# Modulation chunks 4 to 9 placed between the tiles of the gate projection and in the chunk loop of the recurrence

## What is computed

```python
mod_lat = jax.nn.silu(c) @ w_ada[l] + b_ada[l]        # 6 x 1024 values; the same for c_ctx
sh1, sc1, g1, sh2, sc2, g2 = jnp.split(mod[:, None, :].astype(x.dtype), 6, axis=-1)
h = rms_norm(x, lw['norm_pre1']) * (1 + sc1) + sh1
proj = h @ lw['w_in']                                 # hy, q, k, v, og, lr
...
la_f = jax.nn.log_sigmoid(lrf[..., :GLA_RANK] @ w2_f + b_f) / GLA_GATE_NORM
o_f, s_f = gla_scan(qh, kh, vh, la_f, s0_f)           # and backwards
o = rms_norm(o_f + o_b[:, ::-1], gnorm)
o = o.reshape(B, L, GLA_VAL) * jax.nn.silu(og)
...
mix = jnp.concatenate([y_hy, y_gla], axis=-1) @ lw['w_out']
x = x + g1 * rms_norm(mix, lw['norm_post1'])
h2 = rms_norm(x, lw['norm_pre2']) * (1 + sc2) + sh2
```

## Time and profile before

| | us |
|---|---|
| median of 3 runs | 2315.78 |
| lowest and highest of the 3 | 2309.94, 2328.16 |
| the profiled execution, its own time | 2312.32 |
| the profiled execution, its span in the trace | 2310.5 |

### The profile page before, as it was taken

One profiled execution on the slowest core, in us unless ns is written; L12 is line 12 of the kernel. 1 busy time (PEld: TensorE's weight loads), 2 busy tenths in 40 slices (PEclk: granted clock), 3 DMA queues, 4 the chain that ended last, 5 costly groups with the idle time before them and its releaser, 6 DMA issues.

```text
span 2310.5 us, 30679 instructions
## 1 busy us (share of the span) xinstructions
PE 2174.2 (94%) x9868; PEld 1663.6 (72%) x9868; DVE 1439.6 (62%) x3055; ACT 624.0 (27%) x930; POOL 797.5 (35%) x713
## 2 busy tenths in 40 slices
PE   6999989598998899999989999999999999999998
PEld 2554444445997787787868777787888888888886
DVE  4222322623889999788868877324766666666665
ACT  2111022233212222333323323223322323223232
POOL 0000001002323555799979999101221222212210
PEclk8999998798999999999999999999999999999999
DMA  9122134105102444599988999755988888888883
GB/s 339 41 73 73 42 109 153 64 35 191 62 13 96 155 141 136 165 292 296 301 268 288 302 284 301 233 202 184 359 287 289 292 285 294 287 287 294 285 292 145
DMA packets 293477, 475.54 MB, mean 206 GB/s; under 512 B 148871, under 2 KB 150055, under 8 KB 292872
## 3 DMA queue, kind: packets, MB, share of 16 engines
q1 hardware_dynamic: 256520, 340.20, 44.6%
q0 software_dynamic: 36864, 134.23, 16.4%
HBM read 401.76 MB, written 72.61 MB: 205 GB/s over the span
## 4 chain that ended last, share of the span: by engine, by line
PE 64%; POOL 9%; DVE 5%; issue 2%; DMA 2%; ACT 1%; SPq 1%; DVEq 0%; ACTq 0%; POOLq 0%
PE ps L959 30%; PE ps L900 19%; POOL eB L1846 6%; PE ps L837 3%; POOL ugat L1815 3%; PE ps L872 2%; PE ps L873 2%; PE ps L940 2%; PE ps L719 1%; SPq L523 1%; DMA ugat<-in_u_rows,idx 1%; DMA uraw<-in_u_t 1%; PE ps L861 1%; PE ps L819 0%; DVE h2T L1293 0%
## 5 line engine op out<-in xcount | busy, mean ns | idle before, releaser
L900 PE MATMUL ps<-h2hi,uhi 128*128 128x512 f32 x1024 | 449.1, 439 | 23.4 <-POOL ulo L1803 8.3
L900 PE MATMUL ps<-h2hi,ulo 128*128 128x512 f32 x1024 | 405.5, 396 | 0.0
L959 PE MATMUL ps<-vhi,whi 128*128 128x512 f32 x1024 | 399.8, 390 | 5.2 <-DVE wlo L1467 5.2
L900 PE MATMUL ps<-h2lo,uhi 128*128 128x512 f32 x1024 | 403.6, 394 | 0.0
L959 PE MATMUL ps<-vlo,whi 128*128 128x512 f32 x1024 | 399.7, 390 | 0.0
L959 PE MATMUL ps<-vhi,wlo 128*128 128x512 f32 x1024 | 399.5, 390 | 0.0
L1823 POOL DMA_INDIRECT vgat<-in_v_tab,idx x128 | 149.8, 1170 | 654.7 <-DVE y L1477 504.8
L1846 POOL TENSOR_SCALAR eB<-iota,jcur 128x128 f32<-128x128 f32 x384 | 315.9, 836 | 15.9 <-DVE jcur L1432 14.0
L1465 DVE TENSOR_TENSOR vlo<-vraw,vhi 128x1024 fp32r<-128x1024 f32 x128 | 156.8, 1225 | 216.3 <-ACT vhi L1739 216.3
L1739 ACT ACTIVATE vhi<-vraw 128x1024 fp32r<-128x1024 f32 x128 | 135.5, 1061 | 464.4 <-PE ps L959 462.0
L940 PEld LDWEIGHTS ps<-eA,eB 128*128 128x128 f32 x1024 | 189.8, 189 | 90.0 <-POOL eB L1846 29.9
(11 more groups left out here) (270 smaller groups left out, 2908.7 us busy)
## 6 DMA issues: line engine op xcount, KB each, us to landing
uraw<-in_u_t SPq DMA_DIRECT2D x128, 512.0 KB
vraw<-in_v_tab SPq DMA_DIRECT2D x128, 512.0 KB
gelu_scratch<-aout SPq DMA_DIRECT2D x128, 256.0 KB
gate_scratch<-gst SPq DMA_DIRECT2D x16, 2048.0 KB
ain<-gelu_scratch SPq DMA_DIRECT2D x128, 256.0 KB, 4.2
gin<-gate_scratch SPq DMA_DIRECT2D x128, 256.0 KB, 4.4
wring<-in_w_ada SPq DMA_DIRECT2D x12, 2048.0 KB, 7.8
wring<-in_w_in SPq DMA_DIRECT2D x6, 2048.0 KB, 8.4
```

The lines of the kernel that those rows point to most:

```text
L900: last = pe.matmul(ps[:, b % 4, :], w[:, b % 2, k, :], h[:, k, LP:T], start=(k == 0 and j == 0), stop=(k == KD - 1 and j == 2))
L959: last = pe.matmul(ps[:, y_bank(t) + h, :], w[:, b, (t - 1) * P:t * P], v[:, b, h * 512:(h + 1) * 512], start=(start and j == 0), stop=(st ...
```

## The change

On PE the six chunks no longer stand in one block ahead of the gate projection. Chunks 4 and 5 stay where they were, followed by two tiles of the gate projection, the columns of 4 and 5, chunks 6 and 7, the other three tiles, and the columns of 6 and 7. Chunks 8 and 9 move to the chunk loop of the recurrence, one behind the attention blocks of chunk 0 and one behind those of chunk 1, and their columns behind those of chunks 2 and 3. The gate projection's weights are loaded two places earlier in the ring. ACT moves the rows of chunks 4 and 5 ahead of its Exp and Ln, those of 6 and 7 behind the second Silu tile, and those of 8 and 9 behind the `kT` moves. DVE takes chunks 8 and 9 inside its masking loop. Since `modrow` is now in use until then, the final state `st_out`, which shared its place, gets another one, which it shares with the top-k values `sval`; so the wait for the store of the state moves from ACT (ahead of chunk 10) to DVE (ahead of the first scores).

```diff
-        st_out = at("st_out", 36, [P, 2, 2, 128])
+        st_out = at("st_out", 196, [P, 2, 2, 128])
...
-        loads += [("ada", i) for i in range(ADA_1, ADA_2)] + [("in", W_OG), ("out", 0), ("out", 512)]
+        loads += [("ada", 4), ("ada", 5), ("in", W_OG)] + [("ada", i) for i in range(6, ADA_2)] + [("out", 0), ("out", 512)]
...
@@ TensorE @@
-            for i in range(ADA_1, ADA_2):
-                ada(i)
-                if i > ADA_1:
-                    ada_cols(i - 1)
-            ada_cols(ADA_2 - 1)
-            by_token("og", ("in", W_OG))
+            ada(4)
+            ada(5)
+            by_token("og", ("in", W_OG), range(2))
+            ada_cols(4)
+            ada_cols(5)
+            ada(6)
+            ada(7)
+            by_token("og", ("in", W_OG), range(2, NT))
+            ada_cols(6)
+            ada_cols(7)
...
                     last.then_inc(bank_full, 1)
+                if c < 2:
+                    ada(8 + c)
+                elif c < 4:
+                    ada_cols(6 + c)
                 if c:
                     chunk_out(c - 1)
@@ VectorE @@
-            for i in range(4, 5):
-                modulation(i)
+            modulation(4)
...
-            for i in range(6, ADA_2):
-                modulation(i)
+            modulation(6)
+            modulation(7)
...
                 dve.wait_ge(am_ready, c + 1)
+                if c >= 3:
+                    modulation(5 + c)
...
             dve.wait_ge(h2lo_ready, NT)
+            dve.wait_ge(stored, 16)
@@ ScalarE @@
+            mod_row(4)
+            mod_row(5)
             act.wait_ge(ax_ready, 1)
             seq(act.activation(eq[:], eq[:], ACT.Exp, scale=-1.0))
             act.activation(eq[:], eq[:], ACT.Ln, bias=1.0).then_inc(ln_done, 1)
-            for i in range(4, 7):
-                mod_row(i)
...
-            for i in range(7, ADA_2):
-                mod_row(i)
             for t in range(NT):
                 move(f"og{t}", og_sb[:, t], func=ACT.Silu)
+                if t == 1:
+                    mod_row(6)
+                    mod_row(7)
             for c in range(NT):
                 move(f"kT{c}", keT[:, c].rearrange("p j n -> p (j n)"))
+            mod_row(8)
+            mod_row(9)
...
-                    if t == ADA_2:
-                        act.wait_ge(stored, 16)
                     mod_row(t)
```

More of the change, by code:

```diff
@@ L260, in bass_hybrid_layer @@
         order += [f"la{j}{s}" for j in range(4) for s in "ps"]
-        for i in range(ADA_1, ADA_2):
-            order += [f"ada{i}"] + ([f"adc{i - 1}"] if i > ADA_1 else [])
-        order += [f"adc{ADA_2 - 1}"]
-        order += [f"og{t}" for t in range(NT)]
+        order += ["ada4", "ada5", "og0", "og1", "adc4", "adc5", "ada6", "ada7", "og2", "og3", "og4", "adc6", "adc7"]
         order += [f"kT{c}" for c in range(NT)]
@@ L267, in bass_hybrid_layer @@
         for c in range(NT):
-            order += [f"at{c}0", f"at{c}1"] + ([f"o{c - 1}"] if c else [])
+            order += [f"at{c}0", f"at{c}1"] + {0: ["ada8"], 1: ["ada9"], 2: ["adc8"], 3: ["adc9"]}.get(c, [])
+            order += [f"o{c - 1}"] if c else []
         order += [f"o{NT - 1}"]
@@ L711, in _, with by_token @@
                      [(wtile(l)[:, k, (c % 4) * P:(c % 4 + 1) * P], hT[:, k, 0:LP], hT[:, k, LP:T]) for k in range(KD)])
-            def by_token(name, l):
+            def by_token(name, l, tiles=range(NT)):
                 wait_w(pe, l)
-                for t in range(NT):
+                for t in tiles:
                     u = f"{name}{t}"
```

## The result

The changed kernel takes 2286.72 us, the median of 6 runs (2281.27 to 2296.66), against 2314.65 us for the kernel before (6 runs, 2308.77 to 2328.16). The ratio is 0.988, with a 95% interval of 0.984 to 0.991. The profiled execution took 2292.26 us.

The account below looks back on a forecast made before the run. PE's program was taken to bound the kernel, with 64% of the chain. The sum -23.85 + 1.8 = -22.0 us, from a middle of 2314, gave 2292 us, range 2284 to 2304.

Parts of the forecast that it names:

- The block, -23.85: PE's stretch from 335.69 us to the kT transposes: 41.73 us instead of 65.58, so transposes start 23.85 us earlier.
- 10.36 holes, 5.5 moved work, 8.0 clock: Split of the 23.85 us: two PE holes, chunks 8 and 9 with columns leaving, and half-clock work running at full clock.
- the first two end by ACT's queue: PE's holes of 8.95 us ahead of chunk 4's columns and 1.41 ahead of chunk 7's are released by ACT.
- Gate weights: Ring load for the first gate tile lands at 334.6 to 338.0 us, wanted at 335.7; cost 0, at worst 2.3.
- Rows 4 and 5 ahead of the Exp: ACT moves these rows in its 9.26 us wait for DVE, ready at 337.8 before the Exp at 338.06; cost 0.
- DVE's new wait: DVE waits for chunk 4's columns before the scans; 3.4 us later, covered by 6.5 us of gate tiles; cost 0.
- The bank of the fifth tile: ACT drains the first gate tile's bank at 367.0 us, PE reaches it at 368.7; thin cover of 1.7 us.
- The chunk loop, +1.8: Behind the transposes, chunks 8 and 9 fit the hole; their columns add 1.8 us, or 2.7 partly at half clock.
- Rival 2: Chunk loop: the shorter hole before the first chunk output keeps PE's clock up; 1.9 us better, 2290; chance 0.12.
- Rival 1: Light chunks and columns between gate tiles drop PE's clock; gain falls to 14 us, time 2300; chance 0.12.
- The signs: Expected trace: transposes at 377 to 378 us, first chunk output 401 to 403, last about 422; no holes before, full clock.
- a gain here should reach the end unchanged: The changed part ends before the expert mixer, everything behind waits for it, and the mixer should keep its length.

Follow-up runs that it names:

- r_again: The changed kernel once more with no edit; median 2292.19 us, ratio 0.989 to the kernel before.
- b_again2: The kernel before, unchanged, traced again; 2327.10 us, with the transposes 77.51 us behind chunk 4's first product.
- act_only: The kernel before with ACT moving the rows of chunks 4 and 5 ahead of its Exp; transposes 77.20 us behind chunk 4's first product.
- clock_fill: The kernel before with nine unread dense products in PE's hole ahead of chunk 4's columns; transposes 77.59 us behind chunk 4's first product.
- act_all: The kernel before with only ACT's order changed: rows 4 and 5 before Exp, 6 to 9 directly behind Ln; transposes 63.27 us behind chunk 4's first product.
- act_late: The changed kernel with two extra ACT copies ahead of the first Silu; transposes 49.05 us behind chunk 4's first product.
- cols_behind: The changed kernel with chunks 8 and 9's columns and DVE additions behind the chunk loop; median 2289.02 us, ratio 0.988 to the kernel before.
- warm: cols_behind plus unread dense PE products ahead of the first chunk output and the gate rows; ratio 0.987 to the kernel before.
- mod4_late: The changed kernel with DVE's addition for chunk 4 behind the subtraction of the means; transposes 46.85 us behind chunk 4's first product.
- warm_again: The same program as warm, run once more; ratio 0.991 to the kernel before.

## Why the prediction was right

**The forecast.** 2292 us, 22 less than before; the stage in the profiled pair shrank by 21.6 (135.35 to 113.78) and the spans differ by 20.0. The timed medians differ by 27.9, more than forecast but inside the range, and on the other side of one per cent, to which I gave 0.37. Over the timed runs of the three sets with several runs of each kernel, the mean of the kernel before is 2319.5 us (28 runs) and that of the changed kernel 2291.4 (12 runs, r_again with them): 28.0, with a standard error of 2.4 worked out from their spreads of 7.8 and 6.7.

**The block, -23.85.** Measured -24.07 in the profiled pair (70.92 to 46.85). The term was right for the execution that I had. For the kernel before in general it was too small: two of four traces have a block of 77.5, and against these the changed kernel gains 31. The mean of the four, 74.2, less the 46.5 of the changed two is 27.7. I read one trace as the kernel, and did not ask whether its clock would come back at 361 every time, so that the match to 0.2 us in the pair is partly luck. In the changed kernel little is left to chance in the block: 45.9 to 46.9 in the six traces that have its order undisturbed.

**How I split it.** The total was right, the split "10.36 holes, 5.5 moved work, 8.0 clock" was not an account of causes. The step "the first two end by ACT's queue" was the true one. Up to chunk 7's columns the kernel before was bound by ACT's row of chunk 7, which stands behind the exponentials, at 31.86 us behind chunk 4 in the first trace, b_again2, act_only and clock_fill alike, with or without the first hole and at either clock. Behind it PE had 39.06 us of work left in the good case (70.92 - 31.86) and 45.65 in the bad one. ACT's order alone removes the bound, but act_all stopped 16.4 us short of the changed kernel: PE then waits for a load and runs at the half clock, and it still has chunks 8 and 9 to do. The tiles between the chunks take away the first two, and the chunk loop takes over the third. That is the sum of act_all's rows; which part of PE's new order does it was not tested by itself.

**The five covers.** Gate weights: no wait in the profiled pair, as forecast, but 0.83, 0.58, 0.82 and 0.62 us ahead of the first tile in r_again, act_late, cols_behind and warm. In these four chunks 4 and 5 ran at the full clock, so PE was there 1.7 us sooner; this lies within the 2.3 us that I gave as the other end. Rows 4 and 5 ahead of the Exp: it started at 338.99, 0.93 us later than before, as chunk 4 did (0.92), cost 0. DVE's new wait: 3.4 forecast, 3.60 measured, worth nothing by mod4_late. Its cover was thinner than I said, though: `qe_ready` came at 374.1 (369.03 + 5.03) and the transposes at 378.1, 4.1 us and not 6.5, because the product took 5.03 us where it took 2.89. The bank of the fifth tile: 1.7 us of cover by the sum, the two copies of 4.69 us less the wait of 2.96 make it 1.7 in act_late. Weights of chunks 6 to 9: no wait.

**The chunk loop, +1.8.** Measured +1.82 in the profiled pair (43.27 to 45.09). Here too the pair was a mild case. I took 2.7 as the worst and gave the clock from 1.9 better to 1.5 worse; the loop of the changed kernel took 49.25 in r_again, of which 12.5 us were at 0.50:

```profile
404.90:417.40 12.50, 12.47 (x49) 0.50 0.21 80
417.40:429.80 12.40, 12.40 (x88) 0.99 0.00 0
```

The mean of the four traces before is 44.4 and of the changed two 47.2, so the term was nearer 2.8. The loops of mod4_late and act_late, whose edits do not touch it, took 48.55 and 47.88 us and point the same way. Rival 2, that the shorter hole keeps the clock up, did not happen in these four traces nor in cols_behind: the clock fell within the hole of 6.55 to 6.57 us each time. Rival 1 did not happen either: from 336 us to the transposes the clock was 1.00 in all seven traces with this order. The swing that the Trainium skill describes under "A second HAM failure mode: psum-queue depth-cycling" (TensorE: Matmul & The Clock Gate) did not show between the gate tiles of this kernel.

**The signs.** The transposes at 378.12, the first chunk output at 402.46 and the last at 422.60 are where I put them. Of the signs of being wrong, the hole ahead of the first gate tile shows in four later traces, as said. The mixer from its first product with u to the end of the span took 1605.1 us before and 1605.4 after in the profiled pair, but 1599 to 1607 over the four traces before and 1611 in r_again. So "a gain here should reach the end unchanged" is true of the pair, and beyond it can be seen only through this scatter.

**The sum.** 27.7 off the block and 2.8 on the loop is 24.9, with the ends of the stage nearly equal. The mean spans of the same traces (four of the kernel before, two of the changed one) differ by less, 19.3 us (2315.4 and 2296.1), mainly because the mixer is 5.2 us longer in the mean of the two changed traces. The 28 us of the timed runs lie 3 above the stage's 24.9, little more than the standard error of 2.4; where they are, if they are anywhere, was not settled.

## What to carry to other kernels

Ask of a wait not only who ended it, but which later wait of the same engine would end at the same moment without it: two holes and a slow clock here hid one bound, and the edits that took away the first hole or a part of the slow clock gained nothing. Try light work between dense work: here it ran at the full clock there and gave ACT and DVE time, where a block of its own behind a hole ran at half. And trace the kernel before more than once: the stretch with holes and light products had two lengths here, 6.6 us apart, and the gain is measured from their mean.

## What the runs showed of the hardware

**DVE and POOL in each other's way.** The gate tiles now leave ACT while DVE multiplies `eq` with q. POOL multiplies four tiles with the norm weights in 8.21 us, 2.05 each, and the fifth, alone, in 1.26. The third row is act_late, where ACT passed the tiles on only after DVE had finished:

```profile
368.19 8.21 POOL L1793 TENSOR_TENSOR og_sb<-og_sb,gnrow 128x512 f32<-128x512 f32 x4 [71.43 <-ACT og_sb L1528]
377.30 1.26 POOL L1793 TENSOR_TENSOR og_sb<-og_sb,gnrow 128x512 f32<-128x512 f32 x1 [0.89 <-ACT og_sb L1528]
...
375.19 4.95 POOL L1795 TENSOR_TENSOR og_sb<-og_sb,gnrow 128x512 f32<-128x512 f32 x4 [74.99 <-ACT og_sb L1528]
```

DVE's two products of 128x1280, all operands fp32 in SBUF, took 5.03 us in that time and 2.89 beside an idle POOL. In mod4_late, where both came 3.8 us earlier, it was again 8.21 and 5.04. In act_late, where they did not meet, POOL took 4.95 for its four and DVE 2.89 for its two in the same program but for ACT's copies. POOL lost 3.2 us over the four (8.21 less 4 x 1.26), about DVE's two products alone (2.89), and DVE lost 2.1, between one and two of POOL's. So it looks as if one stood still while the other ran. The Trainium skill says so of an instruction of DVE with two inputs in SBUF and one of POOL that reads SBUF (SBUF — State Buffer, section "SBUF: two separate sides"): whichever starts first holds the shared pair of ports for its whole instruction, and the other waits. These numbers agree.

**The clock after a hole.** How long the half clock lasts varied in one and the same program: behind the hole of the chunk loop it was 0.53 for 4.24 us in the first trace of the changed kernel and 0.50 for 12.5 in r_again. The first columns between the chunk outputs took 1.05 us in the one and 1.86 in the other.

**The clock without a hole.** In the traces that start early the clock fell although PE had no idle time. In the first trace of the kernel before PE was busy throughout from 325 to 335 us, and the clock was 0.75 from 330 to 331, 0.50 from 331 to 333, and 1.00 again from 334 on; PE was then in the light products of the gate logits (16 rows) and in chunk 4. That is why chunks 4 and 5 took 5.34 us there and 3.64 in b_again2, where it stayed at 1.00. So light work behind dense work is not safe by itself.

**The mixer.** With the same program, its first part took 889 to 897 us in four traces of the kernel before, and 888 to 901 over the 12 traces other than warm and warm_again. That is about as wide as the swing of the stage, which took 135 to 145 us in the kernel before, and nothing in the part that the change touches explains it.
